# First feed-forward chunk of a two-layer encoder in another order: x in four parts, weights from two queues, products by k-step over both tiles

## The reference

```python
def swiglu(h, w_gate, w_up, w_down):
    return (jax.nn.silu(h @ w_gate) * (h @ w_up)) @ w_down
...
for l in range(DEPTH):                       # 2 layers, x is 256 x 1024, float32
    x = x + 0.5 * swiglu(rms_norm(x, ffn1_norm[l]), ffn1_w_gate[l], ffn1_w_up[l], ffn1_w_down[l])
    h = rms_norm(x, mix_norm[l])
    z = h @ w_in[l]                          # q, k, v, p
    a = neighborhood_attention(q, k, v, rpb[l])
    m = multiscale_pool(p, w_pool[l], pool_scale[l])
    x = x + jnp.concatenate([a, m], axis=-1) @ w_out[l]
    x = x + 0.5 * swiglu(rms_norm(x, ffn2_norm[l]), ffn2_w_gate[l], ffn2_w_up[l], ffn2_w_down[l])
return rms_norm(x, final_norm)
```

## Time and profile before

| | us |
|---|---|
| median of 3 runs | 943.60 (943.59 to 944.06) |
| profiled execution, its time | 944.34 |
| profiled execution, its span | 942.4 |
| TensorE matmul busy in the span | 928.2 |
| VectorE busy, ScalarE busy | 551.7, 499.4 |

### The profile page before, as it was taken

How to read it: one execution, slowest core, us unless ns; L and a number is a source line. 1 busy time by engine, 2 the same in 40 slices (tenths; PEclk the granted TensorE clock), 3 DMA queues, 4 the chain that set the end, 5 groups by cost and what they waited for, 6 DMA issues and landing times.

```text
span 942.4 us, 12733 instructions
## 1 busy us (share of the span) xinstructions
PE 928.2 (98%) x4299; PEld 758.2 (80%) x4299; DVE 551.7 (59%) x896; ACT 499.4 (53%) x821; POOL 44.1 (5%) x81
## 2 busy tenths in 40 slices
PE   8999999999999999999999999999999999999996
PEld 6888888887778888888888888888877888888885
DVE  4655455559746655556476455465786474554654
ACT  5554454556637545545465455454665474544542
POOL 1010100010001001001010000000100000000000
PEclk9999999999999999999999999999999999999999
DMA  7867778836244677776475657554544176465531
GB/s 237 290 162 206 213 171 240 290 127 245 91 133 158 210 216 203 179 237 173 120 234 197 206 198 248 187 173 151 179 157 147 56 261 208 154 221 180 176 136 45
DMA packets 123532, 174.66 MB, mean 185 GB/s; under 512 B 8384, under 2 KB 99696, under 8 KB 123248
## 3 DMA queue, kind: packets, MB, share of 16 engines
q1 hardware_dynamic: 117744, 165.70, 52.7%
q0 software_dynamic: 2848, 6.38, 5.7%
q10 hardware_dynamic: 2912, 2.22, 0.7%
HBM read 173.14 MB, written 4.19 MB: 188 GB/s over the span
## 4 chain that ended last, share of the span: by engine, by line
PE 94%; DVE 3%; ACT 2%; issue 1%; DMA 1%; POOL 0%; POOLq 0%; SPq 0%; DVEq 0%
PE ps L985 29%; PE ps L988 28%; PE ps L986 28%; PE ps L1082 2%; DVE w_lo L728 1%; PE ps L995 1%; PE ps L996 1%; PE ps L1196 1%; PE ps L1070 1%; PE ps L1212 1%; PE ps L1224 1%; DMA w_raw<-in_ffn_w_up_dram 1%; DVE xt_lo L742 1%; ACT xt_hi L488 0%; PE ps L1045 0%
## 5 line engine op out<-in xcount | busy, mean ns | idle before, releaser
L985 PE MATMUL ps<-w_hi,xt_hi 128*128 128x512 f32 x856 | 341.7, 399 | 3.0 <-DVE w_lo L728 1.5
L986 PE MATMUL ps<-w_lo,xt_hi 128*128 128x512 f32 x856 | 333.6, 390 | 0.0
L728 DVE SCALAR_TENSOR_TENSOR w_lo<-w_raw,gains,w_hi 128x512 fp32r<-128x512 f32 x416 | 284.7, 746 | 77.2 <-ACT w_hi L473 76.1
L988 PE MATMUL ps<-w_hi,xt_lo 128*128 128x512 f32 x856 | 329.1, 390 | 0.0
L473 ACT ACTIVATE w_hi<-w_raw,gains 128x512 fp32r<-128x512 f32 x408 | 260.6, 713 | 69.6 <-PE ps L988 69.1
L719 DVE TENSOR_TENSOR w_lo<-w_raw,w_hi 128x1024 fp32r<-128x1024 f32 x104 | 122.8, 1222 | 131.2 <-ACT w_hi L466 130.8
L985 PEld LDWEIGHTS ps<-w_hi,xt_hi 128*128 128x128 f32 x856 | 160.8, 188 | 42.2 <-DVE w_lo L728 4.2
L988 PEld LDWEIGHTS ps<-w_hi,xt_lo 128*128 128x128 f32 x856 | 160.7, 188 | 34.5
L986 PEld LDWEIGHTS ps<-w_lo,xt_hi 128*128 128x128 f32 x856 | 161.0, 188 | 30.3
L466 ACT ACTIVATE w_hi<-w_raw 128x1024 fp32r<-128x1024 f32 x104 | 104.4, 1052 | 116.3 <-PE ps L988 116.2
L985 PE MATMUL ps<-w_hi,gt_hi 128*128 128x512 f32 x352 | 138.0, 392 | 0.0
(11 more groups left out here) (84 smaller groups left out, 407.3 us busy)
## 6 DMA issues: line engine op xcount, KB each, us to landing
w_raw<-in_ffn_w_down_dram SPq DMA_DIRECT2D x88, 512.0 KB, 4.2
w_raw<-in_ffn_w_gate_dram SPq DMA_DIRECT2D x86, 512.0 KB, 4.0
w_raw<-in_ffn_w_up_dram SPq DMA_DIRECT2D x86, 512.0 KB, 5.2
w_raw<-in_w_in_dram SPq DMA_DIRECT2D x32, 512.0 KB, 5.4
w_raw<-in_w_out_dram SPq DMA_DIRECT2D x16, 512.0 KB, 5.3
bias_scratch<-in_rpb_dram POOLq DMA_DIRECT2D x32, 96.0 KB, 6.3
bias<-bias_scratch POOLq DMA_DIRECT2D x2, 1536.0 KB, 6.8
pool_m<-in_pool_matrix_dram ACTq DMA_DIRECT2D x1, 1024.0 KB, 9.7
```

The costliest lines, as they stand in the source:

```text
L728: nc.vector.scalar_tensor_tensor(w_lo[slot][:, part], w_raw[slot][:, part], g, w_hi[slot][:, part].bitcast(F32), ALU.mult, ALU.subtract).t ...
L985: nc.tensor.matmul(o, hi, wh, start=start, stop=False)
L986: nc.tensor.matmul(o, hi, wl, start=False, stop=False)
L988: last = nc.tensor.matmul(o, lo, wh, start=False, stop=bool(stop))
```

## The change

1. **Loads.** x comes in four parts (t, h) of 256 KB, each with its own semaphore. The gate half of g0 is issued by SP, the up half by ScalarE's queue, by k-step. The order on SP is x(0,0), gate k0, x(1,0), gate k1 to k3, x(0,1), x(1,1), g1 in four parts. On ScalarE's queue the four up parts follow the load of the table for Silu and stand ahead of two of the three loads of gains.
2. **The first down unit** is issued on SP right behind the first chunk's loads, ahead of g0 and g1 of the second chunk.
3. **Transposes of tile 1** go to banks 4 and 5 (`acc(1, h)`), in all six norms, without the wait for `xt_lo` of tile 0.
4. **TensorE's start**: 6 matmuls on zeros and not 8, then `transpose_half(0, 0)` and `transpose_half(1, 0)`, each followed by 2 matmuls on zeros (`FILL`).
5. **Products of slot 0** in the first chunk go by k-step over both tiles, with the second halves of x transposed behind k-steps 1 and 2; two transposes of gains follow; slot 1 goes tile by tile as before.
6. **ScalarE and VectorE** follow that order in `first_norm`; both `squares` come after all of the first chunk's splits.
7. **Head of `ff_stage`**, first stage only: the split of the second chunk's g0 comes before `silu` (ScalarE) and `gate` (VectorE) of the first chunk's tile 0.

```diff
-WARM_UP = 8
+WARM_UP = 6
+FILL = 2
...
+        def xt_bank(t, h):
+            return acc(1, h) if t == 1 else ps[:, 6 + h, :]
+
+        def first_weights(weights, a, m, k0, k1):
+
+            dst = w_raw[FF1["g"][a]][:, :].rearrange("p (k m c) -> p k m c", k=4, m=2)
+            src = weights[m][0, a * 512 + k0 * P:a * 512 + k1 * P, 0:FC]
+            return dst[:, k0:k1, m, :], src.rearrange("(k p) c -> p k c", p=P)
...
+                x_half(0, 0)
+                first_half(0, 0, 0, 1, 0)
+                x_half(1, 0)
                 for k in range(1, 4):
-                    quarter(0, k, k + 1, k)
-                sp.dma_start(resid[:, 1, :], x[0, P:2 * P, :]).then_inc(x_loaded[1], 16)
-                quarter(1, 0, 2, 4)
-                quarter(1, 2, 4, 5)
+                    first_half(0, 0, k, k + 1, k)
+                for t in range(TT):
+                    x_half(t, 1)
+                for q in (4, 5):
+                    for m in range(2):
+                        first_half(1, m, 2 * (q - 4), 2 * (q - 3), q)

             def load_ff(layer, ff, weights, begun=0):
+                if begun:
+                    load_down(layer, ff, weights, 0, ff["d"], 0)
                 for i in range(begun, 2):
                     load_gate_up(layer, ff, weights, i, 0)
                     load_gate_up(layer, ff, weights, i, 1)
-                load_down(layer, ff, weights, 0, ff["d"], 0)
+                if not begun:
+                    load_down(layer, ff, weights, 0, ff["d"], 0)
...
+            act.wait_ge(eps_ready, 1)
+            nc.scalar.activation(table_seed[:, :], eps[:, :], ACT.Silu)
+            for k in range(4):
+                dst, src = first_weights((ffn1_w_gate, ffn1_w_up), 0, 1, k, k + 1)
+                act.dma_start(dst, src).then_inc(first_raw[k], 16)
...
             def first_norm():
                 store_xt_hi(0, 0, 0)
                 act.wait_ge(gains_stored, 1)
-                for k in range(2):
+                first_hi(0, 0, 0)
+                store_xt_hi(0, 1, 0)
+                for k in range(1, 4):
                     first_hi(k, 0, k)
+                first_hi(4, 1, 0)
                 store_xt_hi(0, 0, 1)
+                first_hi(4, 1, 1)
+                store_xt_hi(0, 1, 1)
                 for k in range(2, 4):
-                    first_hi(k, 0, k)
-                for h in range(2):
-                    store_xt_hi(0, 1, h)
-                squares(0, 0)
-                for k in range(4):
-                    first_hi(4 + k // 2, 1, k)
-                squares(0, 1)
+                    first_hi(5, 1, k)
+                for t in range(TT):
+                    squares(0, t)
                 act.wait_ge(gains_stored, 2)
...
-                silu_of(layer, ff, 0, 0)
-                unit_g0(layer, ff, 1)
+                if layer * STAGES + ff["stage"] == 0:
+                    unit_g0(layer, ff, 1)
+                    silu_of(layer, ff, 0, 0)
+                else:
+                    silu_of(layer, ff, 0, 0)
+                    unit_g0(layer, ff, 1)
...
-                gate(layer, ff, 0, 0)
-                unit(layer, ff, g0, 1, gains_from=0)
+                if layer * STAGES + ff["stage"] == 0:
+                    unit(layer, ff, g0, 1, gains_from=0)
+                    gate(layer, ff, 0, 0)
+                else:
+                    gate(layer, ff, 0, 0)
+                    unit(layer, ff, g0, 1, gains_from=0)
...
+                slot = FF1["g"][0]
+                for k in range(4):
+                    cols = slice(k * BANK, (k + 1) * BANK)
+                    high, low = w_hi[slot][:, cols], w_lo[slot][:, cols]
+                    pe.wait_ge(hi_ready[slot], k + 1)
+                    if k == 0:
+                        pe.wait_ge(xt_lo_ready, xt_no(0, 0, 0) + 1)
+                    nc.tensor.matmul(ps[:, 0, :], xt_hi[:, 0, k, :], high, start=k == 0, stop=False)
+                    nc.tensor.matmul(ps[:, 0, :], xt_lo[:, 0, k, :], high, start=False, stop=False)
+                    if k == 0:
+                        pe.wait_ge(xt_hi_ready, xt_no(0, 1, 0) + 1)
+                    nc.tensor.matmul(ps[:, 1, :], xt_hi[:, 1, k, :], high, start=k == 0, stop=False)
+                    wait_split(slot, 0, k + 1)
+                    for t in range(TT):
+                        nc.tensor.matmul(ps[:, t, :], xt_hi[:, t, k, :], low, start=False, stop=False)
+                    if k == 0:
+                        pe.wait_ge(xt_lo_ready, xt_no(0, 1, 0) + 1)
+                    last = nc.tensor.matmul(ps[:, 1, :], xt_lo[:, 1, k, :], high,
+                                            start=False, stop=False)
+                    if k >= 1 and k < 3:
+                        transpose_half(0, k - 1, 1)
+                last.then_inc(g0_used, 1)
+                transpose_gains(1)
+                transpose_gains(2).then_inc(gains_t_ready, 1)
...
-            transpose_resid(0, 0)
-            transpose_gains(1)
-            transpose_gains(2).then_inc(gains_t_ready, 1)
+            for t in range(TT):
+                transpose_half(0, t, 0)
+                for n in range(FILL):
+                    nc.tensor.matmul(ps[:, 1, :], zeros[:, 0:P], zeros[:, :], start=True, stop=True)
```

More of the change, by code:

```diff
@@ L173, in trunk @@
         tables_loaded = sem("tables_loaded")
-        x_loaded = [sem(f"x_loaded{t}") for t in range(TT)]
-        x_half_loaded = sem("x_half_loaded")
+        x_loaded = [[sem(f"x_loaded{t}{h}") for h in range(2)] for t in range(TT)]
         bias_rows_loaded = sem("bias_rows_loaded")
@@ L477, in squares @@
                 if number == 0:
-                    act.wait_ge(x_loaded[t], 16)
-                    if t == 0:
-                        act.wait_ge(x_half_loaded, 16)
+                    for h in range(2):
+                        act.wait_ge(x_loaded[t][h], 16)
                 else:
@@ L711, in _, with split_lo @@
                 nc.vector.memset(seeds[:, slot:slot + 1], 0.0).then_inc(lo_ready[slot], 1)
-            def split_lo(slot, n, gains_of=None, halves=(0, 1)):
+            def split_lo(slot, n, gains_of=None, halves=(0, 1), ks=(0, 1, 2, 3)):
                 for h in halves:
@@ L723, in split_lo @@
                     for k in range(2 * h, 2 * h + 2):
+                        if k not in ks:
+                            continue
                         part = slice(k * BANK, (k + 1) * BANK)
@@ L765, in first_norm @@
                 store_xt_lo(0, 0, 0)
-                split_lo(slots[0], 0, gains_of=(0, 0, 0), halves=(0,))
+                split_lo(slots[0], 0, gains_of=(0, 0, 0), ks=(0,))
+                store_xt_lo(0, 1, 0)
+                split_lo(slots[0], 0, gains_of=(0, 0, 0), ks=(1, 2, 3))
+                split_lo(slots[1], 0, gains_of=(0, 0, 4), ks=(0,))
                 store_xt_lo(0, 0, 1)
[L768 to L771, removed]
+                split_lo(slots[1], 0, gains_of=(0, 0, 4), ks=(1,))
+                store_xt_lo(0, 1, 1)
+                split_lo(slots[1], 0, gains_of=(0, 0, 4), ks=(2, 3))
             def gate(layer, ff, i, t):
@@ L1101, in first_gate_up @@
             def first_gate_up():
-                for a in range(2):
-                    slot = FF1["g"][a]
-                    for t in range(TT):
-                        if a == 0 and t == 1:
-                            transpose_resid(0, 1)
-                        for k in range(4):
-                            wait_split(slot, 0, k + 1)
-                            if k == 0:
-                                pe.wait_ge(xt_lo_ready, 2 * t + a + 1)
-                            cols = slice(k * BANK, (k + 1) * BANK)
-                            last = split_products(
-                                [ps[:, t, :]], xt_hi[:, t, 4 * a + k, :], xt_lo[:, t, 4 * a + k, :],
-                                [w_hi[slot][:, cols]], [w_lo[slot][:, cols]],
-                                (a, k) == (0, 0), (a, k) == (1, 3))
-                        if (a, t) == (0, 1):
-                            last.then_inc(g0_used, 1)
-                        if a == 1:
-                            last.then_inc(gu_ready[t], 1)
+                slot = FF1["g"][0]
@@ new lines, in first_gate_up @@
+                last.then_inc(g0_used, 1)
+                transpose_gains(1)
+                transpose_gains(2).then_inc(gains_t_ready, 1)
+                slot = FF1["g"][1]
+                for t in range(TT):
+                    pe.wait_ge(xt_lo_ready, xt_no(0, t, 1) + 1)
+                    for k in range(4):
+                        wait_split(slot, 0, k + 1)
+                        cols = slice(k * BANK, (k + 1) * BANK)
+                        last = split_products(
+                            [ps[:, t, :]], xt_hi[:, t, 4 + k, :], xt_lo[:, t, 4 + k, :],
+                            [w_hi[slot][:, cols]], [w_lo[slot][:, cols]], False, k == 3)
+                    last.then_inc(gu_ready[t], 1)
```

55 lines of the change are left out of this document (26 added, 29 removed).

## The result

| | median, us | range, us | runs |
|---|---|---|---|
| before | 944.16 | 943.23 to 944.86 | 20 |
| changed | 945.39 | 943.91 to 947.46 | 20 |

The ratio of changed to before is 1.0015, 95% interval 1.0009 to 1.0021: 1.2 us slower by the medians, 1.4 by the ratio. That is a loss that 20 runs can tell, and under the 0.2% that I called "same". The new kernel also scatters over 3.6 us, the old one over 1.6. What follows is read with that in mind.

The account below looks back on a forecast made before the run. TensorE's matmuls bound the kernel, so the second chunk's first 24 matmuls decide: start 23.9, plus 0.1, plus 5.46 gives 29.5 against 28.46, +1.0 us, median 943.6 to 944.6. Range 943.3 to 946.3.

Parts of the forecast that it names:

- same: Whole kernel: differences below about 0.2%, 1.9 us, count as no change.
- likeliest class: Second chunk waits for the split and `gated`, set by g0's landing: +0.4 to +1.8 us, 944.0 to 945.4, chance 0.58.
- The gain by itself: First chunk ends at 20.7 instead of 22.64, 1.9 us; with g1's stall of 0.36, at most 2.3 us.
- The landing sets 20.0 + 3.9: Second chunk's start: g0's load landing at 20.0, then split and `gated`, put TensorE's start at 23.9 us.
- L: Moment when the second chunk's g0 has landed: 20.0 us, 19.3 to 21.1.
- the price: Delay of g0 by the down unit loaded ahead of it: 2.7 to 3.6 us by rates, taken as 3.0 - 0.45.
- no gain: Up parts on ScalarE's queue: little was lost to issuing, DMA share already 0.92, so no gain beyond the half of idle.
- `scaled_ready`: Second chunk's split cannot start before 19.8 us; case that it sets the start or both are early: 0.0 to +0.4, chance 0.17.
- the clock: TensorE's 3.2 us gap before the second chunk drops its clock, slowing matmuls: +2.6 to +4.2 us in all, chance 0.12.
- The rest, at nothing: Second chunk's g1 (hidden by 1.7 us), down unit's split, banks 4 and 5, gains' transposes and loads: no cost.
- The gains' transposes and loads are needed only by the mix stage: Gains' transposes and loads, counted at nothing because only the mix stage needs them.

Follow-up runs that it names:

- first profile: Profiled execution of the changed kernel as first measured, nothing altered: 947.1 us, near the top of its runs.
- gate_first: Changed kernel with part 7 alone undone, silu and gated of tile 0 ahead of the split of the second chunk's g0 again: 942.50 us, 0.9983 of before.
- second profile: The changed kernel timed and profiled once more, nothing altered: median 945.83 us, 1.0017 of before; the profiled execution took 945.91.
- down_back: Changed kernel with part 2 alone undone, first down unit loaded behind the second chunk's g0 and g1 again: 945.92 us, 1.0021 of before.
- gap_filled: Changed kernel with 9 matmuls on zeros added on TensorE between first and second chunk: 944.09 us, 1.0005 of before.
- before_two_queues: Kernel before with the four up halves of the first g0 issued by ScalarE's queue, ahead of two loads of gains: 947.20 us, 1.0027 of before.
- before_split_first: Kernel before with part 7 alone put in, the split of the second chunk's g0 ahead of silu and gated: 945.38 us, 1.0014 of before.

## Why the prediction was right, and where only by luck

**The number.** 944.6 was said from a base of 943.6, +1.0; measured +1.2 (1.4 by the ratio), inside the range and at the upper edge of the likeliest class (944.0 to 945.4). The order of waits is confirmed: `gated` behind the split releases the second chunk (4.09 us after the first `w_hi`, 3.92 predicted), and undoing that order alone turns a loss of 1.2 into a gain of 1.5 us.

**The first chunk.** Its end was predicted at 20.7 and was 21.8 in the first profile, 20.7 in the second, where the chunk's last matmul starts at 20.49. The gain by itself was put at 2.3 us at most; gate_first shows 1.5, most of it by the second queue, from which I had taken no gain. What I left out is the rate: in the first profile the products were 0.43 us apart until 10.4 us.

**The step that failed: "The landing sets 20.0 + 3.9".** L was 18.2 and 18.3, not 20.0, and down_back shows that it does not matter. Two terms were mis-sized. I took the rates of before, 291 to 393 GB/s, for the down unit (the average that I called 291 is 294; the price stays at 3.6 us); behind a full queue it was 397 and 399. From 2.25 to 16.3 us the changed kernel moved 7.75 x 310 + 2.5 x 397 + 3.8 x 399 = 4,911 KB, 775 more than before. Of the down unit's 1,049 KB only 274 were left to delay g0, 0.7 us at 399 GB/s, and 17.45 + 0.7 is the 18.2 measured: the price was 0.7 us where I took 2.55. And I took "no gain" from the second queue because the DMA share was 0.92. The share misled me: engines can be counted busy and still move only 275 GB/s. Issuing from one queue against two is 265 against 310 to 323 GB/s and 1.2 to 1.4 us. The rule that I weighed, that a second issuing engine saves only sequencer time (the Trainium skill, DMA: Bandwidth & Descriptors, Issuing engines are not separate DMA queues), is not contradicted. Its remark that this time is usually small beside the DMA itself does not help here: one queue issues 128 KB every 0.47 us, and at 399 GB/s the DMA engines move them in 0.33.

**The bound that held: `scaled_ready`.** 19.8 was predicted, 19.84 and 18.74 measured. It set the start in both profiles. I gave this case 0.17, with a shift of 0 to 0.4 us. In the second profile that is what the start alone gives: 23.00 against 22.64, with g1's stall of 0.36 won back, is 0.0. In the first it is +1.1, as all came 1.1 us later there. And gap_filled, which keeps the wait and takes out the clock, is 1.0005 (0.9996 to 1.0014) of before.

**The rival that came true as well: the clock.** I gave it 0.12 and it happened in both profiles, and in down_back's: gaps of 2.12 and 2.15 us were enough, where I had bounds of 1.1 and 4.4 from rows. Its price was 1.57, 1.54 and 1.60 us, the low end of my 1.6 to 3.2. In the medians, each against the kernel before of its own set: gate_first -1.5, gap_filled +0.1, changed +1.2 and +1.7. So the first chunk brings 1.5, the wait costs 1.6, and the clock 1.1 to 1.5 (the steps add up to the measured time by construction; they are no second proof of it). My +1.0 is right in size, but I had it from the wait alone, which by gap_filled leaves +0.1: a wait 0.9 us too dear stood in for a clock that I thought unlikely. That the two errors make up for each other is luck. The general statement that I had cited, that an idle array loses its full clock (the Trainium skill, TensorE: Matmul & The Clock Gate, Part 1), is what the rows show.

**"The rest, at nothing"** holds for g1, and the down unit's place costs nothing either (942.46 and 942.50). Banks 4 and 5 were not tried apart. "The gains' transposes and loads are needed only by the mix stage" is true of what uses them and missed the point: before_two_queues shows that their transposes had to leave the place ahead of the first products once their loads stood behind the weights.

What stays open is the full scatter of the changed kernel. The clock explains a part of it. The two profiles, at 947.1 and 945.91 us, differ by 1.1 us in the start of the second chunk; the one with the later first full rate is the later one, but no run changes that moment alone. Why two runs of gap_filled were still at 945.52 and 946.01 is not known; their mean granted clock was 0.998, like that of its fast ones.

## What to carry to other kernels

Put work that frees a buffer for the bottleneck engine (here `silu` and `gated`, 0.9 us together) ahead of work on the same engines that is merely ready to be done (here 3.5 us of splitting). Before reordering the start of a kernel, write down for each engine what its next instruction waits for: a load moved back on one queue can stop another engine, if that engine waits for it ahead of its main work. And a gap of 2 us on TensorE had two prices here, the gap and the slower matmuls behind it; matmuls on zeros removed the second.

## What the runs showed of the hardware that was not expected

- A gap of 2.12 to 2.15 us on TensorE was followed by a granted clock of 0.50 in both profiles of the changed kernel and in down_back's; gaps of 1.1 us in the kernel before and in before_split_first, and one of 1.48 us in the latter (ahead of 8.52 us), were not. 1.5 to 1.6 us were lost behind it.
- The first full rate came at different moments in executions of one kernel: the changed kernel's first profile has products 0.43 us apart until 10.4 us, the second has them 0.24 us apart from 8.3 us on.
- Two issuing queues moved 310 to 323 GB/s from 2.25 to 10 us, one 265 to 275, at a DMA share of 0.93 to 1.01 against 0.88 to 0.92. Behind a backlog, from 10 to 16.3 us in the changed kernel, the rate was 397 to 399 GB/s; in down_back, whose queue held less, it was 304 and 273 in the same windows.
